# Casting the projection's weights on another engine, with two buffers instead of three, and zeroing the gate table one stage earlier

## The reference

```
xn = rmsnorm(x, norm1_g)
qa, ka, va, qb, kb, vb, ga, gb = split(xn @ w_in)      # w_in: 1024 x 4352
oa = stick_breaking_attention(qa, ka, va)
ob = sliding_window_attention(qb, kb, vb, rel_bias, sinks)
x  = x + (sigmoid(ga)*(oa @ w_oa) + sigmoid(gb)*(ob @ w_ob)) @ w_o
t  = rmsnorm(x, norm2_g)
e, g = top16 of 128*128 product keys per head, 8 heads; softmax
h  = gelu(u[e] . t) * g ;  x = x + sum h * v[e]         # 128 experts per token
y  = rmsnorm(x, final_g)
```

## Time and profile before

| | before |
|---|---|
| times | 4026.89, 4031.19, 4031.58 us; median 4031.19 |
| profiled execution | 4026.89 us, its span 4025.2 us |
| PE busy | 3549.7 us (88%) |
| DVE busy | 2617.7 us (65%) |
| POOL busy | 1631.8 us (41%) |
| ACT busy | 841.0 us (21%) |
| DMA | 1201.21 MB, mean 298 GB/s |
| `project` in the span | about 397 to 957 us |
| `window` in the span | about 957 to 1087 us |

### The profile page before, as it was taken

How to read it: one execution, slowest core, us unless ns; L and a number is a source line. 1 busy time by engine, 2 the same in 40 slices (tenths; PEclk the granted TensorE clock), 3 DMA queues, 4 the chain that set the end, 5 groups by cost and what they waited for, 6 DMA issues and landing times. The chain is left out here.

```text
span 4025.2 us, 44686 instructions
## 1 busy us (share of the span) xinstructions
PE 3549.7 (88%) x14147; PEld 2107.2 (52%) x14147; DVE 2617.7 (65%) x5036; ACT 841.0 (21%) x1599; POOL 1631.8 (41%) x1245
## 2 busy tenths in 40 slices
PE   8997878776699999988862899999999999999998
PEld 6445567776457667656651344444444444444443
DVE  0451878883405435344464988888888878888886
ACT  1451211112423444354510000010001000010001
POOL 0000077770000777777773433334333334333331
PEclk9899889887799999999986999999999999999999
DMA  7793399995765656666856999999999999999994
GB/s 256 315 408 146 105 383 407 384 391 210 254 222 185 151 128 160 143 138 116 169 123 250 391 406 388 388 400 405 400 416 403 397 372 400 388 398 388 382 387 186
DMA packets 424246, 1201.21 MB, mean 298 GB/s; under 512 B 150473, under 2 KB 215417, under 8 KB 345337
## 3 DMA queue, kind: packets, MB, share of 16 engines
q0 software_dynamic: 168496, 680.80, 45.8%
q1 hardware_dynamic: 187600, 505.84, 34.2%
q10 hardware_dynamic: 67968, 12.45, 1.9%
HBM read 1127.33 MB, written 72.68 MB: 298 GB/s over the span
## 5 line engine op out<-in xcount | busy, mean ns | idle before, releaser
L2066 POOL DMA_INDIRECT d_ring<-peer_uv,d_idx x512 | 655.4, 1280 | 1087.6 <-DVEq L2120 981.9
L2223 PE MATMUL d_ps<-d_xd,d_u 128*128 128x512 f32 x2048 | 908.5, 597 | 99.9 <-DMA d_u<-u_blocks 81.1
L2234 PE MATMUL d_ps<-d_v,d_a 128*128 128x512 f32 x2048 | 914.1, 600 | 43.3 <-DVE d_a L2126 36.5
L1512 POOL DMA_INDIRECT G<-c_cellg,c_cell x384 | 617.5, 1608 | 436.6 <-DVE c_cellg L1641 233.5
L2118 DVE SCALAR_TENSOR_TENSOR d_acc<-d_ring,d_aw,d_acc 128x1024 f32<-128x1024 f32 x512 | 657.7, 1285 | 102.1 <-DVE d_acc L2118 66.9
L2223 PEld LDWEIGHTS d_ps<-d_xd,d_u 128*128 128x128 f32 x2048 | 391.8, 192 | 596.0 <-issue 584.3
L2234 PEld LDWEIGHTS d_ps<-d_v,d_a 128*128 128x128 f32 x2048 | 393.3, 193 | 545.5 <-issue 544.8
L2106 DVE SCALAR_TENSOR_TENSOR d_ring<-d_ring,d_xn 128x1024 f32<-128x1024 f32 x512 | 605.9, 1221 | 97.3 <-DMA d_qacc<-ys 51.5
L840 POOL DMA_INDIRECT a_x<-peer_uv,a_rowu x128 | 154.2, 1205 | 547.8 <-DVE a_rowv L910 505.3
L2188 ACT ACTIVATE d_ge<-d_h (+1 forms) x256 | 52.0, 203 | 1204.9 <-DVE d_ring L2106 1204.6
L1037 PE MATMUL a_ps<-a_w_low,a_x_high 128*128 128x256 f32 (+1 forms) x704 | 204.3, 290 | 61.7 <-DVE a_w_low L852 45.8
(11 more groups left out here) (360 smaller groups left out, 4134.4 us busy)
## 6 DMA issues: line engine op xcount, KB each, us to landing
c_chunk<-wq SPq DMA_DIRECT2D x128, 512.0 KB, 5.0
d_u<-u_blocks SPq DMA_DIRECT2D x128, 512.0 KB, 18.7
d_v<-v_blocks SPq DMA_DIRECT2D x128, 512.0 KB, 16.5
s_kc<-sb_kT SPq DMA_DIRECT2D x32, 1024.0 KB, 9.5
s_vc<-sb_v SPq DMA_DIRECT2D x32, 1024.0 KB, 7.4
c_chunk<-w_m SPq DMA_DIRECT2D x64, 512.0 KB, 5.5
d_gb<-G SPq DMA_DIRECT2D x32, 1024.0 KB, 34.5
G<-b_zeros SPq DMA_DIRECT2D x32, 768.0 KB, 8.3
```

The costliest lines, as they stand in the source:

```text
L1512: pool.indirect_dma_start(out=grid, out_offset=bass.IndirectOffsetOnAxis(ap=cell[q][:, s:s + 1], axis=0), in_=cell_g[q][:, s:s + 1], in_of ...
L2066: pool.indirect_dma_start(out=ring[:, b], out_offset=None, in_=a["peer_uv"], in_offset=bass.IndirectOffsetOnAxis(ap=idx8[par][:, b:b + 1], ...
L2223: last = nc.tensor.matmul(ps[:, HB + x % 2, :], ub[j][:, k], xd[:, k].rearrange("p t q -> p (t q)"), start=(k == 0), stop=(k == KC - 1))
L2234: last = nc.tensor.matmul(ps[:, VB + c % 4, :], A[u][j][:, q * P:(q + 1) * P], vb[u][j][:, half * 512:half * 512 + 512], start=(j == 0), s ...
```

## The change

- The cast to `w_high` moves from ACT to DVE: `split` now waits for the loaded weights, casts, and subtracts.
- `w_high` and `w_low` have two buffers. SP refills a `wbuf` only when PE has finished the block that used the same half (`mm_done`), instead of after its split.
- `experts_of` stands ahead of `split(3)` instead of behind it.
- The 32 zero stores leave SP's queue in `window` and are issued from ACT's queue in `project`, one ahead of each evacuation from block 0 on; POOL's fill of the zero tile moves with them.
- PE runs the blocks in loops (pairs of blocks) in place of a program written out; in blocks 0 to 5 it takes both token halves of a column slice in turn (j // NG, j % NG), instead of both slices of a token half. The mean-square sums go to banks 0 and 1, so PE first waits for both evacuations of these.
- `rstd`, `row_f` and `aw` get tiles of their own.

```diff
-    BETWEEN, GELU_BLOCK, WB = 20, 7, 3
+    BETWEEN, GELU_BLOCK = 20, 7
...
-        w_high, w_low = sb("a_w_high", [P, WB, KC, BW], F32R), sb("a_w_low", [P, WB, KC, BW], F32R)
+        zeros = sb("a_zeros", [P, 4, FIRST_HOT * P])
+        w_high, w_low = sb("a_w_high", [P, 2, KC, BW], F32R), sb("a_w_low", [P, 2, KC, BW], F32R)
...
                 def refill(b, u):
-                    sp.wait_ge(w_split, b + 1)
+                    sp.wait_ge(mm_done, before(b + 1))
                     sp.dma_start(wbuf[:, u], a["w_in"][b + 2]).then_inc(w_in_s[u], 16)
...
             def _(pool):
+                nc.gpsimd.memset(zeros[:], 0.0).then_inc(zero_done, 1)
...
                 def split(b):
+                    u = b % 2
+                    dve.wait_ge(w_in_s[u], 16 * (b // 2 + 1))
+                    nc.vector.tensor_copy(w_high[:, u], wbuf[:, u]).then_inc(w_high_done, 1)
                     dve.wait_ge(w_high_done, b + 1)
-                    nc.vector.tensor_tensor(w_low[:, b % WB], wbuf[:, b % 2], w_high[:, b % WB].bitcast(F32), ALU.subtract).then_inc(w_split, 1)
+                    nc.vector.tensor_tensor(w_low[:, u], wbuf[:, u], w_high[:, u].bitcast(F32), ALU.subtract).then_inc(w_split, 1)
...
                 pairs_best()
+                experts_of()
                 split(3)
-                experts_of()
                 fetch(0, BETWEEN)
...
-                def cast(b):
-                    act.wait_ge(w_in_s[b % 2], 16 * (b // 2 + 1))
-                    nc.scalar.activation(w_high[:, b % WB], wbuf[:, b % 2], ACT.Copy).then_inc(w_high_done, 1)
-
-                for b in range(3):
-                    cast(b)
+                cleared = [0]
+
+                def clear_gates():
+                    if cleared[0] < P:
+                        act.dma_start(o["G"][cleared[0]:cleared[0] + 4, :, 0:FIRST_HOT * P].rearrange("b p t -> p b t"), zeros[:]).then_inc(zero_st, 16)
+                    cleared[0] += 4
+
+                act.wait_ge(zero_done, 1)
...
                         for j in range(PER_T if b < MIXED else NG):
-                            at = (j % 2 * NG + j // 2 if b < MIXED else j) * TG
-                            out(n0 + j, stage[:, u, at:at + TG], bank[(n0 + j) % 8][:], ACT.Copy, **({"scale": SCALE} if b < 4 else {}))
+                            clear_gates()
+                            out(n0 + j, stage[:, u, j * TG:(j + 1) * TG], bank[(n0 + j) % 8][:], ACT.Copy, **({"scale": SCALE} if b < 4 else {}))
                     if b == MIXED:
                         for t in range(NP):
+                            clear_gates()
...
-                    if b + WB < NBLK:
-                        cast(b + WB)
...
+                act.wait_ge(zero_st, 16 * P // 4)
...
-                for b in range(MIXED):
-                    pe.wait_ge(w_split, b + 1)
-                    for j in range(PER_T):
-                        if b == 0 and j % 2 == 0:
-                            pe.wait_ge(xn_done, j // 2 + 1)
-                        transposed(before(b) + j, b, j % 2, j // 2)
...
+                def pair(i):
+                    for u in range(2):
+                        pe.wait_ge(w_split, 2 * i + u + 1)
+                        for j in range(PER_T):
+                            if isinstance(i, int) and i + u == 0 and j < NG:
+                                pe.wait_ge(xn_done, j + 1)
+                            transposed(PER_T * (2 * i + u), PER_T * u, u, j)
+
+                pe.wait_ge(rms_done, NG)
+                pair(0)
+                with pe.Fori(1, MIXED // 2) as i:
+                    pair(i)
...
+                with pe.Fori(VALUES // 2, NBLK // 2) as i:
+                    natural_mm(2 * i + 1, 1)
+                    natural_mm(2 * i + 2, 0)
...
-                sp.wait_ge(zero_done, 1)
-                clear_gates(0, 8)
...
                         load_v(t + 1, 1 - u)
-                        clear_gates(32 + 16 * t, 4)
...
-                sp.wait_ge(zero_st, 16 * P // 4)
...
-                nc.gpsimd.memset(zeros[:], 0.0).then_inc(zero_done, 1)
```

More of the change, by code:

```diff
@@ L745, in project @@
         ring = x_sb
+        rstd = sb("a_rstd", [P, TG])
         g1 = sb("a_g1", [P, KC])
@@ L982, in _ @@
                     act.wait_ge(ms_done, g + 1)
-                    nc.scalar.activation(rms[:, g], bank[6 + g][:, 0:TG], ACT.Sqrt, bias=eps[:]).then_inc(rms_done, 1)
+                    nc.scalar.activation(rms[:, g], bank[g][:, 0:TG], ACT.Sqrt, bias=eps[:]).then_inc(rms_done, 1)
                 def out(n, dst, src, func, **more):
@@ L1027, in _ @@
                     for k in range(KC):
-                        last = nc.tensor.matmul(bank[6 + g][:], mean_w[:], sq[:, k], start=(k == 0), stop=(k == KC - 1))
+                        last = nc.tensor.matmul(bank[g][:], mean_w[:], sq[:, k], start=(k == 0), stop=(k == KC - 1))
                     last.then_inc(ms_done, 1)
@@ L1041, in free @@
                 def free(n):
-                    if n >= 8:
+                    if not (isinstance(n, int) and n < 8):
                         pe.wait_ge(evac, n - 7)
[L1044 to L1051, removed]
@@ L1053, in _, with transposed @@
-                for b in range(MIXED):
-                    pe.wait_ge(w_split, b + 1)
-                    for j in range(PER_T):
-                        if b == 0 and j % 2 == 0:
-                            pe.wait_ge(xn_done, j // 2 + 1)
-                        transposed(before(b) + j, b, j % 2, j // 2)
+                def transposed(n0, at, u, j):
+                    free(n0 + j)
+                    s, tok = j // NG, slice((j % NG) * TG, (j % NG + 1) * TG)
+                    sums(bank[at + j][:], lambda part, k: w_parts[part][:, u, k, s * P:(s + 1) * P], lambda part, k: x_parts[part][:, k, tok])
@@ L1059, in _ @@
                 pe.wait_ge(w_split, MIXED + 1)
                 n0 = before(MIXED)
-                for g in range(NG):
-                    transposed(n0 + g, MIXED, 0, g)
+                for j in range(NG):
+                    transposed(n0, 0, 0, j)
                 for t in range(NP):
                     free(n0 + NG + t)
-                    sums(bank[(n0 + NG + t) % 8][:, 0:P], lambda part, k: x_parts[part][:, k, t * P:(t + 1) * P], lambda part, k: w_parts[part][:, MIXED % WB, k, P:2 * P])
@@ L1066, in _, with natural_mm @@
-                for b in range(VALUES, NBLK):
+                    sums(bank[(n0 + NG + t) % 8][:, 0:P], lambda part, k: x_parts[part][:, k, t * P:(t + 1) * P], lambda part, k: w_parts[part][:, 0, k, P:2 * P])
+                def natural_mm(b, u):
                     pe.wait_ge(w_split, b + 1)
@@ L1069, in _ @@
                         free(before(b) + t)
-                        sums(bank[(before(b) + t) % 8][:, 0:BW], lambda part, k: x_parts[part][:, k, t * P:(t + 1) * P], lambda part, k: w_parts[part][:, b % WB, k])
+                        sums(bank[(before(VALUES) + t) % 8][:, 0:BW], lambda part, k: x_parts[part][:, k, t * P:(t + 1) * P], lambda part, k: w_parts[part][:, u, k])
+                with pe.Fori(VALUES // 2, NBLK // 2) as i:
+                    natural_mm(2 * i + 1, 1)
+                    natural_mm(2 * i + 2, 0)
     return used
@@ L1116, in _ @@
                     sp.dma_start(dst, src).then_inc(tabs, 16)
-                def clear_gates(first, n):
-                    for k in range(n):
-                        sp.dma_start(o["G"][bass.ds(first + 4 * k, 4), :, 0:FIRST_HOT * P].rearrange("b p t -> p b t"), zeros[:]).then_inc(zero_st, 16)
                 def load_qk(t, u):
```

12 lines of the change are left out of this document (5 added, 7 removed).

## The result

The changed kernel takes 4072.3 us (median of 4 runs, 4064.4 to 4076.7) against 4031.4 us (median of four runs of the kernel before): ratio 1.0099, 95% interval 1.0080 to 1.0118, so it is slower by about 41 us, where 33 was forecast. The profiled execution took 4073.55 us (its span 4071.9), 46.7 more than that of before, where 35.5 was forecast.

The account below looks back on a forecast made before the run. It took the DMA as the bound while u rows are gathered, DVE for v rows; 4.5 + 42 + 2.6 + 8.4 - 22 = +35.5 us on 4026.9 gave 4062.4, stated as 4064 us, range 4036 to 4088.

Parts of the forecast that it names:

- The sign, the size and the range: Whole kernel: slower at 84%, 4064 us, range 4036 to 4088 us.
- Start: Start of project: block 2's weight load waits for PE's block 0, DVE stalls 3.2 us, gathers begin 4.5 us later.
- Stores: Project, u rows' gathers: 21 zero stores at 2.0 us each cannot run beside the gathers, +42 us.
- Casts: Project, DVE: seven casts of blocks 10 to 16 add 8.4 us; those of blocks 4 to 9 nothing, at most 7.2.
- The starved gathers: Rival, u rows: POOL can't issue during cast and subtract, six blocks lose up to 3.5 us each, +21 us; chance 10%.
- Two buffers: Project: loads of block b+2 land before DVE asks, no wait; one extra weight load in u rows, 2.6 us.
- Loops: PE in project: a branch per two blocks, hidden in PE's waits for `w_low`, no cost.
- Window: Stage `window`: without zero stores in SP's queue, q and k loads leave earlier, 22 us less.
- The bias: Start of `window`: the second bias load no longer has eight zero stores ahead of it, 4 us sooner.

Follow-up runs that it names:

- a2: Kernel before with only the zero stores moved, one ahead of each evacuation in project, none in window; casts on ACT, three buffers: ratio 1.0036.
- a1: Changed kernel with the 32 zero stores put back on SP's queue in window, all else kept: ratio 1.0087.
- a3: Changed kernel with its zero stores issued earlier, all meant to be out before the first gather: ratio 1.0042.
- a4: Changed kernel with the weight casts back on ACT, among the evacuations of the block before: ratio 1.0070.
- b2: Kernel before with only the weight casts moved from ACT to DVE, ahead of each subtract: ratio 1.0045.
- d1: Kernel before with DVE doing the subtract of splits 4 to 16 twice, casts staying on ACT: ratio 1.0059.
- g1: b2 with two buffers for the split weights instead of three, refill waiting for PE's end of a block: ratio 1.0079.
- c1: Changed kernel with PE's two loops written out, all else kept: ratio 1.0073.
- b1: Kernel before with the zero stores issued early in project on ACT's queue, casts on ACT, three buffers: ratio 0.9986.

## Why the prediction was right, and where it was not

The sign, the size and the range held. That the stores outweigh what `window` gives back, where the DMA is full, was the mechanism, and a2 shows it. But the sum came out so near by some luck: casts and buffers cost more than forecast, stores and window together less, and these errors cancelled.

- **Start.** Forecast +4.5, the trace +3.0. The mechanism (load behind PE's block 0, then a stall) is there, with 2.67 us for 3.2.
- **Stores.** The count of 21 was right. Their price was right in a kernel that keeps the DMA full: a2's 20 cost 37.7 us. In the changed kernel it was mis-sized. By the totals, after minus a1, stores and window together are +5 us (0.0012, give or take 0.0030), where 42 - 22 = +20 stood; alone (a2) they are +14.5. By the traces u is 250.1 with the stores and 226.6 without (a1), 23.5 us instead of 42, but the spread of a1's u makes this number weak. What fits both: without stores, casts and two buffers leave u 16 to 25 us longer (a3, a1), with holes in which the DMA is not full, and the stores run in these holes.
- **Casts.** The term was 8.4 us, and some 3.6 in the start (three casts). In the changed kernel it held: a4 gets back 12 us, 9.3 of it in v and 1.2 in u. The step behind it, "where DVE has 30.9 - 25.3 = 5.6 us of room a block for 1.2 us: nothing, as long as the DMA is the bound", is not sound in general: alone (b2) the casts cost +18 us (12 to 25), and d1's subtracts lengthen u. DVE's pauses were not idle room: where they go, POOL's issue takes 1.98 us instead of 0.98, and then it depends on loads and stores beside the gathers whether the DMA stays full. The term's own upper bound, 7.2 us more, would have been the value to take for b2. The v rows gave +5.2 to 8.5 for six casts in the stretch, as forecast, and block 16's cast 3.7 behind it.
- **The starved gathers.** This rival was given 10% and 21 us. Slow issues and falls of the DMA are there, but its condition was not quite right: POOL is slowed not by cast and subtract alone but also by DVE's row work where it runs without a pause, and its price was not reached (12.5 us in b2, 1.2 in a4). The Trainium skill ("SBUF — State Buffer", section "SBUF: two separate sides") names the copy as what holds the port; the trace shows 2.72 us beside the subtract and 1.98 beside the two-input multiply. The kernel before, where no cast ran on DVE, has an issue of 2.67 us too, beside the subtract at 544.1 us.
- **Two buffers.** "No wait" was right from block 4 on. But g1 is 14 us above b2, where only 2.6 us and a part of the start stood. Where the rest lies stays open.
- **Loops.** Forecast at nothing. c1 neither confirms nor excludes it.
- **Window.** Forecast -22, the trace -23.9, and -23 in a2, a3 and b1. Three of PE's four waits for k are gone; the first tile's is left. The bias was no part of it: DVE's wait for it is 19.9 us (before, 19.28), so its 4 us did not come, and the tiles gave 23.9 where 18 stood.

In a chain of single steps, before, b2, g1, a1, after, the totals are casts 18, buffers 14, loops with order 3 (give or take 12), stores with window 5. That they add up to 40 us follows from the chain and proves nothing; in another order a step has another size. The stores with window are 14.5 when added first (a2) and 5 when added last, the casts 18 first (b2) and 12 last (a4): causes that each empty or fill the same DMA do not add.

## What to carry to other kernels

"The full resource hides the rest" holds only while what feeds it is not slowed by what it hides. Look at how long the feeder's issues take (here POOL's, 0.98 or 1.98 us) in the moments in which the other engine has no pause, and at whether other transfers lie beside these moments. Where none does, take the other engine's added time at full price. Transfers moved to another place cost by how full the DMA is there, and a place counts as free only if the issuing engine can be held up without harm: 16 stores at once held ACT for 25 us. When several causes are added, undo each alone and all but each: here the sum was nearer than its terms.

## What was not expected of the hardware

- A gather's issue on POOL has levels: 0.94 to 0.98 us mostly, where DVE pauses between rows, 1.98 us mostly where it does not, 2.72 us across a cast and a subtract. Beside zero stores there is more in between (median 1.38 us in after, 1.45 in a2, where DVE pauses more than before); why is open. The middle level brings the DMA from 409 to 234 GB/s, if no load or store runs beside the gathers.
- The cast of 128x2048 takes 1.22 us on DVE and 1.91 us on ACT.
- `decide`, with the same instructions in each kernel, took 991.5 to 1001.9 us in 14 profiled executions; its waits were alike, and the granted clock fell below 1.0 at other moments. Why was not settled.
